# Pooling branch of a decoder layer: input projected channel-major, window sums by shifted additions on VectorE, stored rows transposed back

## The chip, the cores and the metric

One core of a Trainium2 chip runs the whole kernel. The metric is the device time of one execution in microseconds. The kernel before took 1297.56 us (median of 3 runs, 1297.35 to 1298.0).

## The reference, cut to what matters

One decoder layer over 264 token rows (256 of a prompt, 8 single-token samples), D = 1024, float32:

```
h = rmsnorm(x);  z = h @ w_in                       # q, f, v, g, u, gate_a, gate_b, 1024 columns each
u -> ext = [15 older rows (zero for the prompt) ; u]
for group g, window w in (2, 4, 8, 16), 256 channels each:
    d  = sum(last w rows of ext) / min(pos + 1, w) - u
    y_pool = (d @ w_pool[g]) * pool_scale
merged = sigmoid(gate_a) * o + sigmoid(gate_b) * y_pool       # o: output of the HGRN2 heads
x += merged @ w_out;  x += top-4-of-32 experts(rmsnorm(x));  x += gated embedding;  final rmsnorm
new_pool = the last 15 rows of ext                            # an output of its own
```

## The kernel before, in words

Each engine has one instruction stream, written out by hand, and semaphores tie them. `bank_jobs` lists every use of the eight PSUM banks in the order in which TensorE (`pe`) fills them, with the engine that drains each ("a" ScalarE, "v" VectorE). `wait_filled` waits for a place in that order, `begin` for the drain of the bank's user before, `wait_drained` for the count of drains of one engine. Where `step` is used, VectorE or GpSimd waits for its own instruction before the next.

The weights `w_in` come as 14 chunks of 512 columns (2 MB each) into four slots. q and f are projected channel-major (L751: weights stationary, 264 tokens moving). The others are projected token-major (`chunk`, L705: 128 tokens stationary, 512 columns moving; `sample_rows`, L728: the 8 sample rows, in four column groups of bank 4). In the stretch that the change touches, TensorE does in order:

- four `state_steps` (L816), beside each of which stand up to four k-steps of the two `u` chunks (L826), and the eight `o` products (L835, L844);
- the last k-step of the u chunks and `gb` chunk 0 (L705), the sample rows of u and gb in one call with 512 columns (L728), `gb` chunk 1 (L705);
- `dT` (L863 to L865): for each of eight channel blocks, u rows times a band matrix of 1/w weights minus identity gives the pooled difference, channel-major; a third product with `selw` adds the sample rows and their 15 older rows (`bufrows`). Each dT bank is copied out by ScalarE or VectorE (L1457, L1786);
- `yp` (L873, L884): dT times `w_pool`; then the transposes `mT` of the merged rows (L666 by `turn_rows`), the product with w_out for the samples (L912), for tile 0 (L905) and for tile 1 (L929), the router, and the experts.

GpSimd makes the constants, the band matrices too (L542 to L551), and only then issues the eight loads of the sample state, `s0` (L564). Later it multiplies sigmoid(gate_b) by pool_scale, one instruction for each of three tiles (L604), once ScalarE has drained gb chunk 1. VectorE waits for all three (L1788), then for each tile in the order samples, 0, 1 multiplies the yp banks by gb (L1794) and adds to og (L1796), which releases that tile's mT.

SyncE's queue issues the weight loads in a fixed order. Expert weights are pieces ("granules") of 1 MB in a ring of 16; `load_first` waits for `s_used`, which TensorE raises as it is done with memory: eight times in dT (L863), four times in the transposes of tile 1, six in L973, then with each pair of pieces consumed.

Two experts make a `pair`, 16 pairs in all: gather rows (L1058, L1068), gate and up products, down product (all L1147), combine (L1205).

Of the kernel before, what the change touches and what calls it, by code (L numbers as in the profile page):

```python
# [14 lines left out]
P = 128  # L15
D = 1024
# [37 lines left out]
def bank_jobs():  # L54
# [62 lines left out]
def build(nc, x_prompt, x_sample, p_prompt, p_sample, state_hgrn, state_pool, g_mix, w_in,  # L117
# [14 lines left out]
    with ExitStack() as ctx:  # L132
# [77 lines left out]
        u = rows3(HG)  # L210
# [5 lines left out]
        pscale_b = view(G0, D)  # L216
        wpool = view(G12, 2048).rearrange("p (g k n) -> p g k n", g=4, k=2)
        wout = view(R + 8 * GRAN, 8192).rearrange("p (k n) -> p k n", k=KD)
        band0 = [view(BAND + g * 144, 144) for g in range(4)]
        band1 = [view(BAND + 4 * 144 + g * P, P) for g in range(4)]  # L220
# [85 lines left out]
        s_ust = sem("pooling_rows_stored")  # L306
        s_gbs = sem("pool_gate_scaled")
# [103 lines left out]
        def _(sp):  # L411
# [53 lines left out]
            sp.wait_ge(s_snew, NS)  # L465
            sp.dma_start(wpool, w_pool[0].rearrange("g (k p) n -> p g k n", p=P)).then_inc(ld["wpool"], 16)

            wait_filled(sp, ("o", 1, 1))
# [40 lines left out]
        def _(pool):  # L509
# [31 lines left out]
            for g, w in enumerate(WINDOWS):  # L541
                step(pool.memset(band0[g], 1.0 / w))  # L542
                for t in range(w - 1):
                    pool.memset(band0[g][:, t:t + 1], 1.0 / (t + 1))
                step(pool.memset(band1[g], 1.0 / w))
                for m, n in ((band0[g], 144), (band1[g], P)):
                    step(pool.affine_select(out=m, in_=m, compare_op=ALU.is_ge, fill=0.0, base=0,
                                            pattern=[[1, n]], channel_multiplier=-1))
                    step(pool.affine_select(out=m, in_=m, compare_op=ALU.is_ge, fill=0.0, base=w - 1,
                                            pattern=[[-1, n]], channel_multiplier=1))  # L550
                    step(pool.tensor_tensor(m[:, 0:P], m[:, 0:P], ident, ALU.subtract))  # L551

                m = selw[:, g, :]
                step(pool.memset(m, 1.0 / w))
                step(pool.affine_select(out=m, in_=m, compare_op=ALU.is_ge, fill=0.0, base=-(NS + BUF + 1 - w),
                                        pattern=[[-BUF, 8]], channel_multiplier=1))
                step(pool.affine_select(out=m, in_=m, compare_op=ALU.is_ge, fill=0.0, base=NS + BUF - 1,
                                        pattern=[[BUF, 8]], channel_multiplier=-1))
                step(pool.tensor_scalar(m[0:NS], ident[0:NS, 0:NS], 1.0 / w - 1.0, None, ALU.mult))
# [32 lines left out]
            pool.dma_start(bufrows[NS:P], rows_of).then_inc(ld["bufrows"], 16)  # L592
            pool.dma_start(new_hgrn_prompt[0, 0].rearrange("h k v -> k h v"), state[NCH]).then_inc(s_stst, 16)

            wait_drained(pool, ("u", 0, 1))
            wait_drained(pool, ("u", 1, 1))
            pool.dma_start(new_pool_prompt[0, 0], u[P - BUF:P, 1, :]).then_inc(s_ust, 16)
            wait_drained(pool, ("u", "s", 3))
            pool.dma_start(new_pool_sample[0, :, BUF - 1, :], bufrows[0:NS]).then_inc(s_ust, 16)
# [7 lines left out]
            wait_filled(pool, ("dT", KD - 1))  # L607
# [3 lines left out]
            pool.wait_ge(s_ust, 32)  # L611
# [43 lines left out]
        def _(pe):  # L655
# [167 lines left out]
            beside = [(n, k) for n in range(2) for k in range(KD - 1)]  # L823
# [30 lines left out]
            for name in [("u", n, t) for n in range(2) for t in range(2)] + [("u", "s", 3)]:  # L854
                wait_drained(pe, name)
            pe.wait_ge(ld["bufrows"], 16)
            pe.wait_ge(s_const, 2)
            for c in range(KD):
                name, g = ("dT", c), c // 2
                begin(name)  # L860
                o, cc = job_bank(name), slice(c * P, (c + 1) * P)

                pe.matmul(o[:, 0:144], u[:, 0, cc], band0[g], start=True, stop=True, skip_group_check=True).then_inc(s_used, 1)  # L863
                pe.matmul(o[:, P:SEQ], u[:, 1, cc], band1[g], start=False, stop=True, skip_group_check=True)
                ins = pe.matmul(o[:, SEQ:T], bufrows[:, cc], selw[:, g, :], start=True, stop=True)  # L865
                fill_done(ins, name)
            pe.wait_ge(ld["wpool"], 16)
            for c in range(KD):
                wait_drained(pe, ("dT", c))
            begin(("yp", 2, 0))  # L870
            for k in range(2):
                for g in range(4):
                    ins = pe.matmul(piece(("yp", 2, g)), dT[:, 2 * g + k, toks(2)], wpool[:, g, k, :],  # L873
                                    start=(k == 0), stop=(k == 1))
                    if k == 1:
                        fill_done(ins, ("yp", 2, g))
# [417 lines left out]
        def _(act):  # L1294
# [126 lines left out]

            for t in range(2):
# [10 lines left out]
            act.wait_ge(s_qm, 1)  # L1433
            copy_out(("u", 0, 0), u[:, 0, halves(0)], job_bank(("u", 0, 0))[:, :])
            copy_out(("u", 1, 0), u[:, 0, halves(1)], job_bank(("u", 1, 0))[:, :])
# [14 lines left out]
            for j in range(4):  # L1450
                name = ("u", "s", j)
                wait_filled(act, name)
                dst = bufrows[0:NS, halves(j)] if j < 2 else gb[0:NS, 2, halves(j % 2)]
                drain_done(act.activation(dst, bank[4][32 * j:32 * j + NS, :], ACT.Copy if j < 2 else ACT.Sigmoid), name)
            pool_gate(1)
            for c in range(0, KD, 2):
                copy_out(("dT", c), dT[:, c, :], job_bank(("dT", c))[:, 0:T])  # L1457
# [130 lines left out]
        def _(dve):  # L1588
# [183 lines left out]
            dve.wait_ge(s_qm, 1)  # L1772
            copy_out(("u", 0, 1), u[:, 1, halves(0)], job_bank(("u", 0, 1))[:, :])
            copy_out(("u", 1, 1), u[:, 1, halves(1)], job_bank(("u", 1, 1))[:, :])

# [9 lines left out]
            for c in range(1, KD, 2):  # L1785
                copy_out(("dT", c), dT[:, c, :], job_bank(("dT", c))[:, 0:T])  # L1786
# [289 lines left out]
```

## Time and profile before

| | us |
|---|---|
| median of 3 runs | 1297.56 |
| profiled execution, its own time | 1297.42 |
| span of its trace | 1295.7 |
| TensorE matmul busy | 1225.1 (95% of the span) |
| TensorE weight loads busy | 554.1 (43%) |
| VectorE / ScalarE / GpSimd busy | 331.4 / 175.2 / 73.8 |
| loaded from memory | 455.00 MB, 356 GB/s over the span |

The span is counted from the first to the last record; the execution's own time is 1.72 us longer. A time such as 249.13 below is counted in us from the start of the span. A matmul of float32 stands as two instructions in the trace. Busy time of pipelined matmuls overlaps, so durations of TensorE work are best read from one start to the next.

### The profile page before, as it was taken

What the parts mean: (1) busy time and instruction counts of PE and PEld (TensorE: products, weight loads), DVE (VectorE), ACT (ScalarE), POOL (GpSimd) and SP (SyncE); (2) the same over time, 40 slices, a digit from 0 to 9 for tenths busy, and PEclk for the clock granted to TensorE, in tenths of its full rate; (3) what the DMA queues carried; (4) which work ended last, traced back from release to release, by engine and by line L of the source; (5) the groups of instructions that cost most, each with busy time, mean ns of one, the idle gap of its engine ahead of it and who ended that gap; (6) DMA issues with size and microseconds to landing.
All of it is one profiled execution on the core that took longest, in us unless ns stands there. A gap on an engine that the chain in (4) does not pass through costs nothing.

```text
span 1295.7 us, 15572 instructions
## 1 busy us (share of the span) xinstructions
PE 1225.1 (95%) x6203; PEld 554.1 (43%) x6203; DVE 331.4 (26%) x648; ACT 175.2 (14%) x435; POOL 73.8 (6%) x168
## 2 busy tenths in 40 slices
PE   7999999999999999999898999989898989999996
PEld 6855445556333343433334343433333343434333
DVE  3155344133311212212121221211121212212223
ACT  3136203121100100001010000000010100001022
POOL 8021020210000000000000000000000000000001
PEclk9999999999999999999999999999999999999998
DMA  9847272595889999999999999999999999999961
GB/s 333 291 144 252 82 285 83 201 375 223 358 355 422 422 420 421 421 422 422 422 422 422 422 422 422 422 423 422 422 422 422 422 422 422 422 421 422 420 263 36
DMA packets 80051, 461.55 MB, mean 356 GB/s; under 512 B 8181, under 2 KB 9377, under 8 KB 31112
## 3 DMA queue, kind: packets, MB, share of 16 engines
q1 hardware_dynamic: 74512, 445.18, 84.0%
q0 software_dynamic: 3424, 11.28, 2.8%
q10 hardware_dynamic: 2072, 4.49, 1.1%
q8 instruction: 30, 0.49, 0.2%
q14 instruction: 13, 0.11, 0.0%
HBM read 455.00 MB, written 6.39 MB: 356 GB/s over the span
## 4 chain that ended last, share of the span: by engine, by line
PE 74%; DMA 22%; DVE 2%; issue 1%; SPq 0%; ACT 0%; POOLq 0%; POOL 0%; DVEq 0%; ACTq 0%
PE bank L1147 37%; DMA arena<-in_w_down_dram 19%; PE bank L705 11%; PE bank L1205 5%; PE bank L751 4%; PE bank L1058 3%; PE bank L1241 2%; DMA arena<-in_w_up_dram 2%; PE bank L1068 1%; DMA arena<-in_w_ple_gate_dram 1%; PE bank L728 1%; PE bank L1168 1%; PE bank L929 1%; PE bank L905 1%; DVE arena L1961 1%; PE bank L1076 1%
## 5 line engine op out<-in xcount | busy, mean ns | idle before, releaser
L1147 PE MATMUL bank<-arena 128*64 128x512 f32 x3072 | 679.1, 596 | 37.8 <-DMA arena<-in_w_up_dram 24.6
L1147 PEld LDWEIGHTS bank<-arena 128*64 128x64 f32 x3072 | 222.9, 137 | 475.2 <-issue 472.5
L705 PE MATMUL bank<-arena 128*128 128x512 f32 x320 | 140.0, 595 | 0.0
L705 PEld LDWEIGHTS bank<-arena 128*128 128x128 f32 x320 | 60.0, 190 | 74.6 <-issue 73.9
L1973 DVE TENSOR_TENSOR arena<-bank,arena 128x512 f32<-128x512 f32 (+1 forms) x96 | 61.6, 682 | 75.5 <-PE bank L1205 75.3
L1205 PE MATMUL bank<-arena 128*128 128x512 f32 (+1 forms) x192 | 74.6, 601 | 0.9 <-DVE arena L1966 0.9
L1058 PEld LDWEIGHTS bank<-arena 128*128 128x128 f32 x512 | 62.7, 196 | 25.4 <-issue 25.2
L1955 DVE TENSOR_SCALAR arena<-bank 128x512 f32<-128x512 f32 x32 | 20.6, 686 | 196.6 <-PE bank L1147 196.6
L1966 DVE COPY arena<-bank 128x512 f32<-128x512 f32 x16 | 11.1, 692 | 230.7 <-PE bank L1147 230.7
L1058 PE MATMUL bank<-arena 128*128 128x128 f32 x512 | 68.8, 288 | 0.0
L1937 DVE TENSOR_SCALAR arena<-bank 128x512 f32<-128x512 f32 x32 | 20.6, 686 | 182.6 <-PE bank L1147 182.6
L751 PE MATMUL bank<-arena 128*128 128x264 f32 x256 | 57.2, 386 | 0.6 <-DVE arena L1631 0.6
L1489 ACT ACTIVATE arena<-arena 128x1024 f32<-128x1024 f32 x16 | 16.9, 1057 | 281.2 <-DVE arena L1937 281.2
L635 POOL TENSOR_SCALAR arena<-arena 128x1 f32<-128x1 f32 (+1 forms) x3 | 0.7, 219 | 944.2 <-ACT arena L1524 944.2
L751 PEld LDWEIGHTS bank<-arena 128*128 128x128 f32 x256 | 48.6, 190 | 8.9 <-ACT arena L1349 0.7
L1474 ACT ACTIVATE arena<-bank,arena 128x128 f32<-128x128 f32 x124 | 33.7, 382 | 54.9 <-PE bank L1068 54.9
L1205 PEld LDWEIGHTS bank<-arena 128*128 128x128 f32 (+1 forms) x192 | 24.7, 155 | 38.0 <-issue 36.2
L1503 ACT ACTIVATE arena<-bank 128x512 f32<-128x512 f32 x16 | 9.6, 597 | 231.5 <-PE bank L1147 231.5
L1501 ACT ACTIVATE arena<-bank 128x264 f32<-128x264 f32 x16 | 6.3, 391 | 249.3 <-PE bank L1191 249.3
L1241 PE MATMUL bank<-arena 128*8 128x256 f32 (+2 forms) x144 | 31.7, 452 | 1.7 <-DMA arena<-in_w_ple_gate_dram 1.7
L1076 PE MATMUL bank<-arena 128*128 128x128 f32 x128 | 19.6, 296 | 11.5 <-DVE arena L1961 11.5
L1940 DVE TENSOR_TENSOR arena<-arena 128x1024 f32<-128x1024 f32 x16 | 19.6, 1225 | 19.1 <-ACT arena L1489 19.1
(253 smaller groups left out, 705.1 us busy)
## 6 DMA issues: line engine op xcount, KB each, us to landing
arena<-in_w_gate_dram SPq DMA_DIRECT2D x128, 1024.0 KB, 26.5
arena<-in_w_up_dram SPq DMA_DIRECT2D x128, 1024.0 KB, 26.5
arena<-in_w_down_dram SPq DMA_DIRECT2D x126, 1024.0 KB, 26.1
arena<-in_w_in_dram SPq DMA_DIRECT2D x14, 2048.0 KB, 12.4
out_dram<-arena POOLq DMA_DIRECT2D x9, 512.0 KB, 5.2
arena<-in_state_hgrn_dram POOLq DMA_DIRECT2D x8, 512.0 KB, 12.7
arena<-sample_values ACTq DMA_DIRECT2D x8, 512.0 KB, 7.2
arena<-in_w_out_dram SPq DMA_DIRECT2D x4, 1024.0 KB, 8.0
```

The costliest lines, as they stand in the source:

```text
L705: ins = pe.matmul(job_bank(name)[:, :], hT[:, k, toks(t)], w[:, k, :], start=(k == 0), stop=(k == KD - 1))
L751: ins = pe.matmul(job_bank((kind, h))[:, 0:T], w_slot[c % NSLOT][:, k, (h % 4) * P:(h % 4 + 1) * P], hT[:, k, :], start=(k == 0), stop=(k ...
L1058: ins = pe.matmul(XG[k // 4][:, (k % 4) * P:(k % 4 + 1) * P], h2[:, t, every_other(k)], oh[:, t, :], start=(k % 4 == 0 and t == 0), stop=F ...
L1076: ins = pe.transpose(out[c][:, j * P:(j + 1) * P], src[:, every_other(k)], ident)
L1147: ins = pe.matmul(out[c][hp(one), :], src[:, k * P + CAP * one:k * P + CAP * one + CAP], w[one][:, j, halves(c)], start=(first and k == 0) ...
L1205: ins = pe.matmul(out, comb[:, toks(t)], y_sb[:, halves(c)], start=True, stop=True)
L1241: ins = pe.matmul(gate_piece(r, t, n), xT[:, k, toks(t)], gran[k // 2][:, k % 2, gate_cols(t, n)], start=(k == 0), stop=(k == KD - 1))
L1474: ins = act.activation(xT_e[:, k * P:(k + 1) * P], bank[6 + c][:, (k % 4) * P:(k % 4 + 1) * P], ACT.Copy, scale=gffn[:, k:k + 1])
L1937: ins = dve.tensor_scalar(g_sb[:, halves(c)], bank[c][:, :], LIMIT, None, ALU.min)
L1940: dve.tensor_tensor(g_sb, g_sb, sig_sb, ALU.mult).then_inc(s_dloop, 1)
L1955: ins = dve.tensor_scalar(u_sb[:, halves(c)], bank[2 + c][:, :], LIMIT, -LIMIT, ALU.min, ALU.max)
L1973: ins = dve.tensor_tensor(xs, src, xs, ALU.add)
```

## The change

- The `u` chunks are computed channel-major: eight `uT` jobs, each 8 matmuls of 128x264 as for q and f, two of them beside each `state_steps`; ScalarE copies each to `uT` with 16 columns of room ahead of it. `sample_rows` is called for gb alone, with 256 columns. The bands, dT matmuls and dT copies are gone.
- New on TensorE, between the sample rows of gb and gb chunk 1: `bs` (eight products of older sample rows with `selw`, 8 columns each) and `ur` (eight transposes of the 23 rows to be stored, back to token-major); ScalarE copies ur out.
- New on VectorE: window sums by additions of shifted copies, 1, 2, 3 and 4 for the four windows, the scaling by 1/w and subtraction of u, the first w-1 columns with their own divisors, and the sample columns.
- yp waits for that chain (`s_pooled`). The first eight expert pieces are released together by the first yp matmul.
- The load of w_pool moves behind `o`; piece 0 no longer waits for L604; the wait for the stored rows moves behind it.
- GpSimd's constants get shorter, and what stands behind them is issued earlier.

```diff
 # bank_jobs
-    for t in range(2):
-        for half in range(2):
-            jobs += [(("dS", t, half, c), 4 + c, "v") for c in range(4)]
+    for n in range(4):
+        jobs += [(("dS", n // 2, n % 2, c), 4 + c, "v") for c in range(4)]
+        jobs += [(("uT", c), c % 4, "a") for c in (2 * n, 2 * n + 1)]
...
-    chunk("u", 0, 0, "av")
-    chunk("u", 1, 1, "av")
     chunk("gb", 0, 0, "aa")
-    jobs += [(("u", "s", j), 4, "a") for j in range(4)]
+    jobs += [(("gb", "s", j), 4, "a") for j in range(4)]
+    jobs.append((("bs",), 5, "v"))
+    jobs += [(("ur", half), 6 + half, "a") for half in range(2)]
     chunk("gb", 1, 1, "aa")
-    for c in range(KD):
-        jobs.append((("dT", c), c % 4, "av"[c % 2]))
 # sync
+            wait_filled(sp, ("o", 1, 1))
             sp.dma_start(wpool, ...).then_inc(ld["wpool"], 16)
...
-            sp.wait_ge(s_ust, 32)
-            for n, at_ in enumerate((1, 2, 3, 4, 5, 6, 15, 16)):
-                load_first(at_, n + 1)
-            sp.wait_ge(s_gbs, NT)
+            for at_ in (1, 2, 3, 4, 5, 6, 15, 16):
+                load_first(at_, 8)
             sp.wait_ge(s_osq, 1)
             load_first(0, 8)
+            sp.wait_ge(s_ust, 32)
 # gpsimd: constants, for each window
-                step(pool.memset(band0[g], 1.0 / w))
+                step(pool.memset(share[:, g, :], 1.0 / w))
                 for t in range(w - 1):
-                    pool.memset(band0[g][:, t:t + 1], 1.0 / (t + 1))
-                step(pool.memset(band1[g], 1.0 / w))
-                for m, n in ((band0[g], 144), (band1[g], P)):
-                    (two affine_select and one tensor_tensor)
+                    pool.memset(share[:, g, t:t + 1], 1.0 / (t + 1))
 # tensor
             for n in range(4):
                 state_steps(n // 2, n % 2)
-                for m, k in beside[4 * n:4 * n + 4]:
-                    chunk_step("u", m, k)
+                for c in (2 * n, 2 * n + 1):
+                    name, w = ("uT", c), w_slot[chunk_no[("u", c // 4)] % NSLOT]
+                    begin(name)
+                    for k in range(KD):
+                        ins = pe.matmul(job_bank(name)[:, 0:T], w[:, k, (c % 4) * P:(c % 4 + 1) * P], hT[:, k, :], ...)
+                    fill_done(ins, name)
...
-            for n in range(2):
-                chunk_step("u", n, KD - 1)
             chunk("gb", 0)
-            sample_rows("u", (10, 11, 12, 13))
-            chunk("gb", 1)
+            sample_rows("gb", (12, 13))
+            begin(("bs",))
             for c in range(KD):
-                (two band products and one with selw)
+                ins = pe.matmul(bank[5][:, c * NS:(c + 1) * NS], bufrows[0:NS * BUF, c * P:(c + 1) * P],
+                                selw[0:NS * BUF, c // 2, :], start=True, stop=True)
+            fill_done(ins, ("bs",))
+            (waits for all uT drains; ur: 8 transposes of uT[:, c, 16 + SEQ - BUF:16 + T] into banks 6 and 7)
+            chunk("gb", 1)
             pe.wait_ge(ld["wpool"], 16)
+            pe.wait_ge(s_pooled, 1)
 # scalar, ahead of the o jobs
+            act.wait_ge(s_snew, NS)
+            for c in range(KD):
+                copy_out(("uT", c), uT[:, c, 16:16 + T], job_bank(("uT", c))[:, 0:T])
 # vector
+            step(dve.memset(uT[:, :, 0:16], 0.0))
+            wait_filled(dve, ("bs",))
+            for g, w in enumerate(WINDOWS):
+                two, src, shift = slice(2 * g, 2 * g + 2), uT[:, 2 * g:2 * g + 2], 1
+                for n in range(g + 1):
+                    lo = 2 * shift - 1
+                    step(dve.tensor_tensor(sums[n % 2][:, :, lo:272], src[:, :, lo:272], src[:, :, lo - shift:272 - shift], ALU.add))
+                    src, shift = sums[n % 2], 2 * shift
+                step(dve.scalar_tensor_tensor(dT[:, two, 0:SEQ], src[:, :, 16:272], 1.0 / w, uT[:, two, 16:272], ALU.mult, ALU.subtract))
+                step(dve.tensor_tensor(src[:, :, 16:15 + w], ..share.., ALU.mult))
+                step(dve.tensor_tensor(dT[:, two, 0:w - 1], src[:, :, 16:15 + w], uT[:, two, 16:15 + w], ALU.subtract))
+                ins = dve.scalar_tensor_tensor(dT[:, two, SEQ:T], uT[:, two, 16 + SEQ:16 + T], 1.0 / w - 1.0, ..bank[5].., ALU.mult, ALU.add)
+            drain_done(ins, ("bs",))
+            dve.memset(stat[:, 30:31], 0.0).then_inc(s_pooled, 1)
```

## Rows read from the trace of the kernel before

**Rows 1.** The page: busy tenths of the DMA engines in 40 slices.

```profile
DMA  9847272595889999999999999999999999999961
```

**Rows 2.** Windows: stretch, length, busy time of each engine, granted clock, DMA share, GB/s.

```profile
290.00:300.00 10.00, 10.00 (x67) 5.52 (x66) 3.56 (x17) 0.00 (x0) 0.00 (x0) 1.00 0.08 32
500.00:1000.00 500.00, 467.89 (x2315) 189.37 (x2313) 103.01 (x153) 35.18 (x90) 0.00 (x0) 1.00 1.01 422
```

**Rows 3.** Timeline of SyncE's queue: start, length, line, what it issues, count.

```profile
249.62 3.74 SPq L434 DMA_DIRECT2D arena<-in_w_gate_dram  x6
302.18 1.98 SPq L434 DMA_DIRECT2D arena<-in_w_up_dram  x4
316.93 17.01 SPq L434 DMA_DIRECT2D arena<-in_w_down_dram  x6
```

**Rows 4.** Timeline of TensorE, 173 to 269 us: start, length, line, shapes, count, idle before.

```profile
174.63 7.13 PE L705 MATMUL bank<-arena 128*128 128x512 f32 x16
181.69 1.17 PE L816 MATMUL bank<-arena 32*128 32x128 f32 x32
199.13 3.27 PE L705 MATMUL bank<-arena 128*128 128x512 f32 x7
202.67 1.05 PE L835 MATMUL bank<-arena 128*128 128x128 f32 x8
210.95 17.43 PE L705 MATMUL bank<-arena 128*128 128x512 f32 x40
228.31 7.05 PE L728 MATMUL bank<-arena 128*8 128x512 f32 x64
235.30 14.00 PE L705 MATMUL bank<-arena 128*128 128x512 f32 x32
249.13 0.41 PE L863 MATMUL bank<-arena 128*128 128x144 f32 x2
255.45 1.05 PE L873 MATMUL bank<-arena 128*8 128x256 f32 x16 [0.72 <-DVE arena L1599]
263.54 1.68 PE L666 MATMUL bank<-arena 8*128 8x8 f32 x16
265.14 3.64 PE L912 MATMUL bank<-arena 128*8 128x256 f32 x64
268.71 1.09 PE L666 MATMUL bank<-arena 128*128 128x128 f32 x8
```

**Rows 5.** TensorE elsewhere: the nearest rows to the new jobs.

```profile
12.58 57.20 PE L751 MATMUL bank<-arena 128*128 128x264 f32 x256 [0.63 <-DVE arena L1631]
303.51 1.94 PE L956 MATMUL bank<-arena 128*128 128x32 f32 x16
```

**Rows 6.** VectorE's groups by form: busy, mean ns of one.

```profile
L1687 DVE TENSOR_TENSOR arena<-arena 128x512 f32<-128x512 f32 x4 | 2.8, 693 | 21.2 <-ACT arena L1380 21.1
L1870 DVE SCALAR_TENSOR_TENSOR arena<-bank,arena 128x32 f32<-128x32 f32 x2 | 0.5, 251 | 1.0 <-PE bank L956 1.0
```

**Rows 7.** Timeline of GpSimd.

```profile
25.30 7.32 POOL L564 DMA_DIRECT2D arena<-in_state_hgrn_dram  x8
250.08 6.97 POOL L604 TENSOR_TENSOR arena<-arena 8x1024 f32<-8x1024 f32 x3 [11.47 <-ACT arena L1447]
```

**Rows 8.** Timeline of VectorE around the merge.

```profile
257.08 1.77 DVE L1794 TENSOR_TENSOR arena<-bank,arena 8x256 f32<-8x256 f32 x4 [1.89 <-POOL arena L604]
258.88 1.22 DVE L1796 TENSOR_TENSOR arena<-arena 8x1024 f32<-8x1024 f32 x1
261.45 1.22 DVE L1796 TENSOR_TENSOR arena<-arena 128x1024 f32<-128x1024 f32 x1
```

**Rows 9.** The window in which the granted clock falls.

```profile
325.00:330.00 5.00, 5.00 (x18) 1.42 (x16) 0.00 (x0) 0.00 (x0) 0.00 (x0) 0.66 0.37 154
```

**Rows 10.** Timeline of TensorE, products of the first pair, outside and inside that stretch.

```profile
313.21 7.09 PE L1147 MATMUL bank<-arena 128*64 128x512 f32 x32
324.80 8.78 PE L1147 MATMUL bank<-arena 128*64 128x512 f32 x32 [1.29 <-ACT arena L1474]
```

More of the change, by code:

```diff
@@ L209, in build @@
         tmp = [view(TMP + n * HALF, HALF) for n in range(2)]
-        u = rows3(HG)
+        uT = view(G0, KD * (T + 16)).rearrange("p (k t) -> p k t", k=KD)
+        sums = [view(BAND, 544).rearrange("p (k t) -> p k t", k=2),
+                view(G0 + KD * (T + 16), 544).rearrange("p (k t) -> p k t", k=2)]
+        share = view(BAND + 1024, 64).rearrange("p (g t) -> p g t", g=4)
+        urows = view(HG + 2048, D, BUF + NS)
         gb = rows3(HG + 3072)
@@ L215, in build @@
         bufrows = view(V, D)
-        pscale_b = view(G0, D)
-        wpool = view(G12, 2048).rearrange("p (g k n) -> p g k n", g=4, k=2)
+        pscale_b = view(V + D, D)
+        wpool = view(HG, 2048).rearrange("p (g k n) -> p g k n", g=4, k=2)
         wout = view(R + 8 * GRAN, 8192).rearrange("p (k n) -> p k n", k=KD)
-        band0 = [view(BAND + g * 144, 144) for g in range(4)]
-        band1 = [view(BAND + 4 * 144 + g * P, P) for g in range(4)]
         h2 = rows3(OG)
@@ L306, in build @@
         s_ust = sem("pooling_rows_stored")
+        s_pooled = sem("pooled_rows_ready")
         s_gbs = sem("pool_gate_scaled")
@@ L822, in _ @@
             wait_chunk(chunk_no[("u", 1)])
-            beside = [(n, k) for n in range(2) for k in range(KD - 1)]
             for n in range(4):
                 state_steps(n // 2, n % 2)
-                for m, k in beside[4 * n:4 * n + 4]:
-                    chunk_step("u", m, k)
+                for c in (2 * n, 2 * n + 1):
+                    name, w = ("uT", c), w_slot[chunk_no[("u", c // 4)] % NSLOT]
+                    begin(name)
+                    for k in range(KD):
+                        ins = pe.matmul(job_bank(name)[:, 0:T], w[:, k, (c % 4) * P:(c % 4 + 1) * P], hT[:, k, :],
+                                        start=(k == 0), stop=(k == KD - 1))
+                    fill_done(ins, name)
             for t in range(2):
@@ L847, in _ @@
                     fill_done(ins, name)
-            for n in range(2):
-                chunk_step("u", n, KD - 1)
             chunk("gb", 0)
-            sample_rows("u", (10, 11, 12, 13))
-            chunk("gb", 1)
-            for name in [("u", n, t) for n in range(2) for t in range(2)] + [("u", "s", 3)]:
-                wait_drained(pe, name)
+            sample_rows("gb", (12, 13))
             pe.wait_ge(ld["bufrows"], 16)
             pe.wait_ge(s_const, 2)
+            begin(("bs",))
             for c in range(KD):
-                name, g = ("dT", c), c // 2
+                ins = pe.matmul(bank[5][:, c * NS:(c + 1) * NS], bufrows[0:NS * BUF, c * P:(c + 1) * P],
+                                selw[0:NS * BUF, c // 2, :], start=True, stop=True)
+            fill_done(ins, ("bs",))
+            for c in range(KD):
+                wait_drained(pe, ("uT", c))
+            for half in range(2):
+                name = ("ur", half)
                 begin(name)
[L861 to L865, printed above, removed]
+                for j in range(4):
+                    ins = pe.transpose(job_bank(name)[0:BUF + NS, j * P:(j + 1) * P],
+                                       uT[:, 4 * half + j, 16 + SEQ - BUF:16 + T], ident)
                 fill_done(ins, name)
+            chunk("gb", 1)
             pe.wait_ge(ld["wpool"], 16)
-            for c in range(KD):
-                wait_drained(pe, ("dT", c))
+            pe.wait_ge(s_pooled, 1)
             begin(("yp", 2, 0))
@@ L874, in _ @@
                                     start=(k == 0), stop=(k == 1))
+                    if k == 0 and g == 0:
+                        ins.then_inc(s_used, 8)
                     if k == 1:
@@ L1420, in _ @@
             gate_chunk("ga", 1)
+            act.wait_ge(s_snew, NS)
+            for c in range(KD):
+                copy_out(("uT", c), uT[:, c, 16:16 + T], job_bank(("uT", c))[:, 0:T])
             for t in range(2):
@@ L1450, in _ @@
             for j in range(4):
-                name = ("u", "s", j)
+                name = ("gb", "s", j)
                 wait_filled(act, name)
-                dst = bufrows[0:NS, halves(j)] if j < 2 else gb[0:NS, 2, halves(j % 2)]
-                drain_done(act.activation(dst, bank[4][32 * j:32 * j + NS, :], ACT.Copy if j < 2 else ACT.Sigmoid), name)
+                drain_done(act.activation(gb[0:NS, 2, cols(2, j)], bank[4][32 * j:32 * j + NS, 0:256], ACT.Sigmoid), name)
+            for half in range(2):
+                name = ("ur", half)
+                copy_out(name, urows[:, halves(half)], job_bank(name)[0:BUF + NS, :])
             pool_gate(1)
-            for c in range(0, KD, 2):
-                copy_out(("dT", c), dT[:, c, :], job_bank(("dT", c))[:, 0:T])
             turned("mT", mT, ORD)
```

46 lines of the change are left out of this document (20 added, 26 removed).

## The prediction

> **What bounds the kernel now.** Read first the DMA line of the page [rows 1]: from the thirteenth slice on (some 390 us) the DMA engines are always busy. The windows say it sharper [rows 2]: over 500 us in the experts the DMA share is 1.01 at 422 GB/s while TensorE is busy 467.89, so it waits for weights. The experts are bound by the stream of pieces, whose bytes the change leaves alone. But before the stream closes up it has gaps: from 290 to 300 us the DMA share is 0.08 with TensorE busy all of the time [rows 2], and SyncE issues the next pieces at 302.18 and 316.93 only because TensorE has come that far [rows 3]. Up to there TensorE's order of work sets the time; whatever it is earlier at the product after the pooling (265.14, L912), the stream and the end are earlier too. So the timeline of TensorE from 173 to 269 us [rows 4] is what has to be worked out anew, and the two engines that release its merged rows, GpSimd and VectorE [rows 7, 8].
>
> **The change part by part, TensorE up to the end of gb chunk 1.**
> - u as uT. One uT job is 16 of the instructions of L751, 57.20 / 256 = 0.223 us each [rows 5]; the pair of jobs beside a `state_steps` takes 32 x 0.223 = 7.15 us. The four k-steps that stand there now take 181.69 - 174.63 = 7.06 [rows 4]. Three times +0.09: +0.27. Beside the fourth there are two k-steps now, 202.67 - 199.13 = 3.54; in their place 7.15: +3.61. The u k-steps behind the o products go: 228.31 - 210.95 = 17.36 less a chunk of 235.30 to 249.13 = 13.83, so -3.53.
> - Sample rows. 64 instructions of 512 columns take 235.30 - 228.31 = 6.99; with 256 columns the same count is 3.6 (L912, from 265.14 to 268.71 it is 3.57) [rows 4]: -3.42.
> - bs. 16 instructions with 128x128 weights and 8 columns. No such row stands alone. The nearest has 32 columns: 1.94 us for 16 [rows 5], that is 1.8 without the last one's tail. At least half of that, and at most one of L705's slots each (13.83 / 32 = 0.43, 6.9 in all) bound it; I take +1.8.
> - ur. Eight transposes; eight of 128x128 take 1.09 with their tail [rows 4]. Between 0.5 and 2.2 for 23 rows out instead of 128; I take +1.0.
>
> The sum is +0.27 + 3.61 - 3.53 - 3.42 + 1.8 + 1.0 = -0.3: gb chunk 1 ends at 248.8 instead of 249.13. The banks that uT takes (0 to 3) are drained by ScalarE, which has no other job between ga chunk 1 and o; its copies come in pairs, one pair in some 8 us. So the new work on TensorE replaces the old one for one, and what is gained lies behind gb chunk 1.
>
> **Behind gb chunk 1.** dT and the wait for its last copy go: 255.45 - 249.13 = 6.32 us [rows 4]. yp can start at 248.8, if VectorE's chain is done, and as it took 263.54 - 255.45 = 8.09, it ends at 256.9.
>
> **VectorE's chain** starts when bs is filled, at 248.8 - 13.83 - 1.0 = 234.0. It has 10 additions of two blocks (542 to 514 elements, mean 536), each 536 / 512 x 0.693 = 0.725 [rows 6]: 7.25. Four scalings with subtraction, 512 elements, 0.70 each: 2.8. Twelve small ones at the 0.25 of L1870 [rows 6]: 3.0. Each waits for the one before; the gap between dependent ones is 0.03 (257.08 + 1.77 to 258.88) [rows 8], 27 times 0.9. Sum 14.0, so the pooled columns are ready at 248.0, 0.8 us before TensorE asks. Gb chunk 1 and the ur transposes (14.8 us) hide it; in the order written, VectorE has no other work there. Without that cover it would cost all of its 14 us. Bounds: 10 us, if the small ones cost nearly nothing, and 21 if a wait of a step costs 0.3.
>
> **What is late next.** The merge. GpSimd begins L604 at 250.08, when ScalarE has drained gb chunk 1, and takes 6.97 us for its three tiles [rows 7]; VectorE waits for it even now, 1.89 us, and starts at 257.08 [rows 8]. None of this moves but with the end of gb chunk 1, by 0.3. So VectorE starts at 256.8, releases the sample tile at 256.8 + 1.77 + 0.03 + 1.22 = 259.8, and tile 0 at 261.45 + 1.22 - 0.34 = 262.3, as by then the yp banks have long been full. TensorE, done at 256.9, waits 2.9 us, turns the sample rows in 0.6, waits until 262.4, and turns tile 0 in 1.0. L912 starts at 263.4 instead of 265.14: **1.7 us** of the 6.6 are left. Tile 1's merge (two banks and one addition, about 2.6 us) is done at 265, before L912 ends at 267; behind that, the order and the distances are those of before.
>
> **The queues.** w_pool (1 MB) is loaded behind o instead of at 174; yp comes over 30 us later: nothing. In SyncE's queue it stands ahead of w_out only by its issue. The first eight pieces are issued now from 249.62 on [rows 3], one by one with dT, and afterwards in one burst when yp has begun, at 249; piece 0 follows without waiting for L604. The gap of 290 to 302 shows 11 us of slack before the next ones are due, which are asked for 1.7 earlier: nothing. The stored rows go out over GpSimd's queue around 237, with 6 us until piece 7 needs them gone and no engine waiting behind them but L604, 12 us later. The load of bufrows is issued when o has been drained, now 3.6 us later (some 218); bs asks at 232: nothing. The constants of GpSimd shorten: `s0` is issued at some 12 us instead of 25.30 [rows 7]; as TensorE is held by nothing but its own work from 12.58 on, no gain; the risk is a rival.
>
> The sum against the profiled execution is 1297.42 - 1.7 = 1295.7; the median of the three runs is 0.14 above that execution, so I forecast **1295.8 us**.
>
> **The rivals.**
 The new stretch, 256.9 to 262.4, has 4.9 us of waiting in 5.5, and L912 behind it has only 8 columns per group. Against it: the transposes and L912 run there today at full clock. If it falls, and lasts as long as at 325, half of it lies in the stall: 0.9 to 1.7 lost, 1296.7 to 1297.5. **The slower end of it:** if the low clock stays for all of mT 0, L912 and mT 1 (1.0 + 3.6 + 1.0), it costs 5.6, and the time is 1297.5 + 3.9 = 1301.4. It decides for slower from a loss of 1.7 us. The Trainium skill (TensorE: Matmul & The Clock Gate, The HAM clock gate) says that idleness of the array lowers its clock and sustained work restores it; by that rule the fall in this stall is the expected case.
> 2. *The dip at 325 goes away*, since all of it is shifted by 1.7 us against whatever decides it. That gives back 1.7 more: 1294.1. For: it is one dip, after one short wait of 1.29 [rows 10]. Against: the three runs lie within 0.65 us, so it is not a thing of chance.
> 3. *GpSimd's scaling does not hold the merge* (VectorE starts as soon as yp is full): all 6.6 come off, 1290.9. Against it stands the wait of 1.89 for L604 [rows 8].
> 4. *VectorE's chain is too long.* TensorE's yp may start up to 251.7 without any loss, since the merge holds it anyway, and has lost all gain at 255.4: a chain of 21 us where I count 14. From there on slower, up to 1298. By the Trainium skill (SBUF — State Buffer, Who interferes with whom), a VectorE instruction with two SBUF inputs and a GpSimd one lock each other out. No row here shows it, as they do not overlap now; by my sum the chain ends 1.7 us before L604 starts.
> 5. *The earlier s0 loads (4 MB) starve w_in.* The second chunk of q is due at 12.58 + 14.3 = 26.9. If it comes later by more than 1.7 the kernel gets slower; say 2 to 4 us late, 1298 to 1300. Against it: even if all of s0 went first, the input tiles (1 MB), two chunks and s0 are 9.4 MB, 22 us at the 422 GB/s of [rows 2], behind the start of the loads near 1 us. It is close only if the small pieces of s0 move much slower: unlikely, and the later chunks have 14 us more each.
>
> **How the numbers follow.** The forecast has a chance of 0.42, the first rival 0.28, the second 0.14, the third 0.04, the fourth 0.04, the fifth 0.04, other things 0.04. What the measurement can tell from no change is about 0.2%, 2.6 us: below 1295.0 is faster, above 1300.2 slower. Faster: the second and third rival and the low edge of the first case (0.04), 0.21. Slower: the tail of the first rival 0.05, of the last ones 0.04, 0.09. Same: 0.70. The range, 1293.6 to 1299.2, takes in the second rival and the first up to a loss of 3.4, and leaves out the third and the far tails.
>
> **What would show it right or wrong.** In the changed trace: L912's counterpart starts at about 263.4; the last gb chunk ends within 1 us of 248.8; TensorE has two waits for VectorE's merge of 2.9 and 2.0 us, and VectorE one for GpSimd ahead of it; the three GpSimd scalings still take 2.34 each; the chain on VectorE lasts 14 us and yp waits less than 1 for it; the granted clock is 1.00 from 255 to 275. It is wrong if L912 starts later than 264.5, if the stream of pieces does not close up earlier by what L912 gained, or if a wait appears before 173 us.

## The result

The changed kernel took 1301.63 us (median of 18 runs) against 1298.12 for the kernel before (18 runs, 1297.35 to 1299.94). Seventeen of the 18 lie between 1298.45 and 1304.0, and a single slow one of 4454.66 is left out of the ratio, which is 1.002 with a 95% interval of 1.0013 to 1.0028. The two medians alone are 3.5 us (0.27%) apart. It is slower by 0.2 to 0.3%. The forecast was 1295.8 with a range to 1299.2: wrong in sign, and outside the range. The profiled execution took 1301.44 us with a span of 1299.7, 4.0 more than before.

### The profile page after: what moved, and what is told of

Its sections match the earlier page's. It is cut to its first block, busy times and chain, and to the rows that moved or that the text cites. A ratio compares the mean times of both kernels' runs of the same rounds, so it can differ in the third digit from the quotient of the medians.

```text
span 1299.7 us, 15644 instructions
## 1 busy us (share of the span) xinstructions
PE 1224.4 (94%) x6243; PEld 565.8 (44%) x6243; DVE 340.3 (26%) x670; ACT 175.8 (14%) x439; POOL 63.0 (5%) x136
## 4 chain that ended last, share of the span: by engine, by line
PE 73%; DMA 22%; DVE 2%; POOL 1%; issue 1%; SPq 1%; ACT 0%; POOLq 0%; DVEq 0%; ACTq 0%
PE bank L1139 36%; DMA arena<-in_w_down_dram 19%; PE bank L692 9%; PE bank L1197 5%; PE bank L738 5%; PE bank L1050 3%; PE bank L1233 2%; PE bank L816 2%; DMA arena<-in_w_up_dram 2%; PE bank L1060 1%; DMA arena<-in_w_ple_gate_dram 1%; PE bank L1160 1%; PE bank L715 1%; PE bank L921 1%; PE bank L897 1%; DVE arena L1970 1%
## 5 line engine op out<-in xcount | busy, mean ns | idle before, releaser
L1139 PE MATMUL bank<-arena 128*64 128x512 f32 x3072 | 678.8, 596 | 38.0 <-DMA arena<-in_w_up_dram 24.8
L692 PE MATMUL bank<-arena 128*128 128x512 f32 x256 | 111.4, 594 | 0.0
L692 PEld LDWEIGHTS bank<-arena 128*128 128x128 f32 x256 | 48.1, 190 | 59.9 <-issue 59.6
L1050 PEld LDWEIGHTS bank<-arena 128*128 128x128 f32 x512 | 62.7, 196 | 25.4 <-issue 25.2
L738 PE MATMUL bank<-arena 128*128 128x264 f32 x256 | 59.3, 396 | 0.6 <-DVE arena L1623 0.6
L738 PEld LDWEIGHTS bank<-arena 128*128 128x128 f32 x256 | 50.0, 196 | 9.6 <-issue 0.7
L1289 ACT ACTIVATE arena<-bank 128x512 f32<-128x512 f32 (+4 forms) x32 | 15.0, 484 | 111.6 <-PE bank L816 30.6
```

The lines of the kernel that those rows point to most:

```text
L692: ins = pe.matmul(job_bank(name)[:, :], hT[:, k, toks(t)], w[:, k, :], start=(k == 0), stop=(k == KD - 1))
L738: ins = pe.matmul(job_bank((kind, h))[:, 0:T], w_slot[c % NSLOT][:, k, (h % 4) * P:(h % 4 + 1) * P], hT[:, k, :], start=(k == 0), stop=(k ...
L1050: ins = pe.matmul(XG[k // 4][:, (k % 4) * P:(k % 4 + 1) * P], h2[:, t, every_other(k)], oh[:, t, :], start=(k % 4 == 0 and t == 0), stop=F ...
L1139: ins = pe.matmul(out[c][hp(one), :], src[:, k * P + CAP * one:k * P + CAP * one + CAP], w[one][:, j, halves(c)], start=(first and k == 0) ...
```

## The profile after

The page of the changed kernel, its busy times and granted clock in 40 slices:

```profile
PE 1224.4 (94%) x6243; PEld 565.8 (44%) x6243; DVE 340.3 (26%) x670; ACT 175.8 (14%) x439; POOL 63.0 (5%) x136
PEclk9999999989999999999999999999999999999999
```

TensorE is as busy as before, GpSimd 11 us less, VectorE 9 more, and the slice from 260 to 292 us has a lower clock (the 8), which it has not in the profile before. The timeline of TensorE (start, length, line, shapes, count, idle before) shows the rest; it answers to [rows 4, 5]:

```profile
13.00 59.29 PE L738 MATMUL bank<-arena 128*128 128x264 f32 x256 [0.63 <-DVE arena L1623]
...
175.98 1.17 PE L803 MATMUL bank<-arena 32*128 32x128 f32 x32 [0.15 <-issue]
177.08 7.39 PE L816 MATMUL bank<-arena 128*128 128x264 f32 x32
184.40 1.17 PE L803 MATMUL bank<-arena 32*128 32x128 f32 x32
...
231.78 3.64 PE L715 MATMUL bank<-arena 128*8 128x256 f32 x64
235.35 1.95 PE L845 MATMUL bank<-arena 120*128 120x8 f32 x16
237.16 1.03 PE L854 MATMUL bank<-arena 128*23 128x128 f32 x8
238.03 13.90 PE L692 MATMUL bank<-arena 128*128 128x512 f32 x32
251.86 1.05 PE L863 MATMUL bank<-arena 128*8 128x256 f32 x16
252.84 7.17 PE L876 MATMUL bank<-arena 128*128 128x256 f32 x32
262.77 0.88 PE L653 MATMUL bank<-arena 8*128 8x8 f32 x8 [2.76 <-DVE arena L1805]
265.35 1.97 PE L653 MATMUL bank<-arena 128*128 128x128 f32 x8 [1.70 <-DVE arena L1805]
267.25 4.89 PE L904 MATMUL bank<-arena 128*8 128x256 f32 x64
272.07 1.09 PE L653 MATMUL bank<-arena 128*128 128x128 f32 x8
```

Three things stand there. The q and f projections (L738) take 2.1 us more than before, 59.22 from the first start to the next group (72.22) against 57.12, and begin 0.4 later. From the first `state_steps` (173.53 before, 175.98 now) to the sample product (265.14, 267.25) it is 91.27 us against 91.61: 0.3 gained, where 1.7 was forecast. And the two waits for the merge (2.76 and 1.70) are followed by work at half speed: the transposes of tile 0 take 1.90 from start to start, the sample product 4.82 where it was 3.57 before. The windows (length, busy times, granted clock, DMA share, GB/s) show the clock there. The kernel before, first, has 1.00 in the same stretch:

```profile
260.00:265.00 5.00, 5.00 (x33) 4.26 (x31) 4.54 (x7) 0.41 (x2) 1.10 (x3) 1.00 1.01 411
265.00:270.00 5.00, 5.00 (x75) 2.78 (x74) 1.73 (x4) 1.49 (x4) 2.97 (x7) 1.00 1.03 379
```

```profile
255.00:260.00 5.00, 5.00 (x24) 4.07 (x22) 0.30 (x1) 0.00 (x0) 5.00 (x4) 1.00 1.02 424
260.00:265.00 5.00, 0.89 (x9) 0.79 (x8) 4.81 (x8) 0.22 (x1) 5.00 (x11) 0.80 1.00 417
265.00:270.00 5.00, 4.65 (x36) 2.61 (x40) 2.71 (x4) 1.19 (x2) 0.00 (x0) 0.52 1.05 321
270.00:275.00 5.00, 5.00 (x53) 2.69 (x46) 1.68 (x4) 2.12 (x4) 0.00 (x0) 1.00 0.99 322
```

The clock has two levels, 1.2 and 2.4 GHz, and 0.80 and 0.52 are means over 5 us. Together they lack 0.20 x 5 + 0.48 x 5 = 3.4 us of full speed. The dip at 325 us in the kernel before [rows 9] lacks half as much, 0.34 x 5 = 1.7.

What holds the merge is, as forecast, GpSimd's scaling (L592), which VectorE awaits for 9.68 us. The first of these lines is the last of VectorE's chain; they answer to [rows 7, 8]:

```profile
249.97 0.06 DVE L1795 MEMSET arena<- 128x1 f32 x1
259.70 1.76 DVE L1803 TENSOR_TENSOR arena<-bank,arena 8x256 f32<-8x256 f32 x4 [9.68 <-POOL arena L592]
261.50 1.21 DVE L1805 TENSOR_TENSOR arena<-arena 8x1024 f32<-8x1024 f32 x1
```

```profile
252.71 6.96 POOL L592 TENSOR_TENSOR arena<-arena 8x1024 f32<-8x1024 f32 x3 [12.54 <-ACT arena L1439]
```

The chain runs from 237.41 to 250.03: 12.6 us, and yp does not wait for it.

## The experiments

**Fill the waits, leave them in place.**

```diff
-            turn_rows("mT", og, ..., tiles=(2, 0))
+            wait_drained(pe, ("gb", 1, 1))
+            for _ in range(5):
+                pe.matmul(bank[3][:, 0:256], ident, hT[:, 0, 0:256], start=True, stop=True)
+            turn_rows("mT", og, ..., tiles=(2,))
+            for _ in range(3):
+                (the same product)
+            turn_rows("mT", og, ..., tiles=(0,))
```

> The changed kernel with dummy products (128x256) in TensorE's two waits for the merge: five before the transposes of the sample rows (2.2 of 2.76 us), three before those of tile 0 (1.3 of 1.70 us). The waits themselves stay. Theory A (the clock falls to 1.2 GHz because of these waits, and the transposes and the sample product run slowly behind them): the clock stays at 1.00 from 255 to 275, the transposes of tile 0 take 1.0 instead of 1.90 and the sample product 3.57 instead of 4.82, the time falls by about 2.1 us to 1299.5. Theory B (the loss is made at the start of the kernel, where the q and f projections take 59.3 instead of 57.2 us since constants are shorter and the state loads earlier): no change, about 1301.6.

Measured: 1298.74 us (12 runs, 1294.46 to 1305.43), against 1299.12 for the kernel before beside it (23 runs), ratio 1.0004 (0.9987 to 1.0021): not told apart from the kernel before. Its timeline of TensorE:

```profile
248.95 1.05 PE L863 MATMUL bank<-arena 128*8 128x256 f32 x16
...
262.43 1.09 PE L653 MATMUL bank<-arena 128*128 128x128 f32 x8 [0.43 <-DVE arena L1811]
263.45 3.64 PE L910 MATMUL bank<-arena 128*8 128x256 f32 x64
267.02 1.09 PE L653 MATMUL bank<-arena 128*128 128x128 f32 x8
```

The merge is no earlier, but the work behind it runs at full speed: 1.02 and 3.57. This is the world that was forecast: gb chunk 1 ends at 248.95 (forecast 248.8) and the sample product starts at 263.45 (forecast 263.4). So the fall of the clock in the stall is caused by TensorE having nothing to do there, and costs 0.9 + 1.25 = 2.1 us. The Trainium skill (TensorE: Matmul & The Clock Gate, The HAM clock gate) says that an idle array loses its clock. The trace agrees: 1.90 and 4.82 us behind the empty waits, 1.02 and 3.57 behind the filled ones.

The other executions say the same. The mean granted clock of a whole execution is 0.998 in 5 of these 12, and never above 0.994 in the 37 comparable executions of kernels that have this merge unfilled.

The time is less clear than the trace. The interval of this ratio overlaps that of the changed kernel (1.0013 to 1.0028), so the expected fall of 2.1 us fits but isn't shown by the times. In this execution the clock fell in the router stretch instead, the thin products between the w_out product and the first pair of experts (windows of the same run, where the kernel before has 1.00):

```profile
300.00:305.00 5.00, 4.90 (x41) 4.27 (x39) 3.20 (x10) 3.61 (x5) 0.90 (x4) 1.00 0.73 247
305.00:310.00 5.00, 5.00 (x22) 4.13 (x21) 3.13 (x11) 0.68 (x3) 1.75 (x6) 0.51 1.00 424
```

**Wait for one tile's scaling at a time.**

```diff
-            dve.wait_ge(s_gbs, NT)
             for t in ORD:
+                dve.wait_ge(s_gbs, ORD.index(t) + 1)
```

> The changed kernel, but VectorE waits only for the scaling of the tile that it merges next, not for all three. Step of the prediction tested: the three GpSimd scalings of 6.97 us hold the merge. Then VectorE starts 4.65 us earlier, both waits of TensorE (2.76 and 1.70) all but go, the sample product starts at about 262 instead of 267.25 and the clock does not fall: some 5.5 us from the waits and 1.3 from its full speed, about 1295. If the clock falls all the same (theory A wrong in its cause): about 1296.5. If the merge is held by something else: no change, 1301.6.

Measured: 1295.05 (12 runs, 1291.17 to 1298.72), ratio to before 0.9968 (0.9956 to 0.9981). By the intervals it is faster than both kernels, by 0.3% against the one before.

```profile
249.04 1.05 PE L863 MATMUL bank<-arena 128*8 128x256 f32 x16
250.02 7.17 PE L876 MATMUL bank<-arena 128*128 128x256 f32 x32
257.12 0.66 PE L653 MATMUL bank<-arena 8*128 8x8 f32 x8
259.03 1.09 PE L653 MATMUL bank<-arena 128*128 128x128 f32 x8 [1.25 <-DVE arena L1805]
260.05 3.64 PE L904 MATMUL bank<-arena 128*8 128x256 f32 x64
```

The scaling did hold the merge. The sample product starts at 260.05, 2 us earlier than expected. That the time still came out at 1295 is in part luck, as in this execution the clock fell in the router stretch (0.65 and 0.67 over 300 to 310). One wait of 1.25 is left, for the most part because VectorE and GpSimd now get in each other's way. GpSimd's three instructions take 7.99 us in place of 6.96, and two of VectorE's additions 1.61 and 1.95 in place of 1.21:

```profile
252.27 1.76 DVE L1803 TENSOR_TENSOR arena<-bank,arena 8x256 f32<-8x256 f32 x4 [5.07 <-POOL arena L592]
254.06 1.61 DVE L1805 TENSOR_TENSOR arena<-arena 8x1024 f32<-8x1024 f32 x1
255.70 1.29 DVE L1803 TENSOR_TENSOR arena<-bank,arena 128x512 f32<-128x512 f32 x2
257.02 1.95 DVE L1805 TENSOR_TENSOR arena<-arena 128x1024 f32<-128x1024 f32 x1
```

**Load the sample state late.** `wait_filled(pool, ("q", 3))` ahead of L554.

> The changed kernel, but GpSimd issues the loads of the sample state only when four q heads are done (at about 28 us, near the 25.3 of before, instead of 17.7). Theory B with the loads as cause: the q and f projections take 57.2 us again and the time falls by about 2 us, to 1299.6. Theory A: no change, about 1301.6; the length of the first q head then varies between executions whatever the loads do.

Measured: 1303.01 (6 runs, 1301.37 to 1304.53), ratio 1.0034 (1.0021 to 1.0046). q and f took 60.13. The slow start is there with the loads late as well, so the early loads are not what slows it.

**Both, with filler in the first pair.** The wait for each tile, and `keep_warm(2, bank[5])` behind `gather_samples((1,))`.

> As the one with a wait for each tile, and with two dummy products of 128x256 in the first expert pair, in TensorE's wait of 1.29 us ahead of which 32 products take 8.6 to 8.8 instead of 7.09 us. If that fall of the clock comes from the wait: 1.6 us less than without them, about 1293.4. If it comes from the thin products before it (128x128 and 8 rows): no difference, about 1295, or 0.2 more where the dummies outlast the wait.

Measured: 1293.67 (6 runs, 1291.56 to 1296.05), ratio 0.9963 (0.9949 to 0.9977). The 32 products take 7.02 from start to start. That alone doesn't show that the filler did it, as they took 7.01 without it in the run with only the wait for each tile. In this one the clock fell behind the short wait of the merge, though it is only 1.23 us:

```profile
258.73 1.09 PE L653 MATMUL bank<-arena 128*128 128x128 f32 x8 [1.23 <-DVE arena L1806]
259.75 5.33 PE L904 MATMUL bank<-arena 128*8 128x256 f32 x64
```

**The same filler at the start, in both kernels.** Eleven products before the first transposes:

```diff
             pe.wait_ge(s_const, 1)
+            for _ in range(11):
+                pe.matmul(bank[6][:, 0:P], ones, ident, start=True, stop=True)
```

> The kernel before, with 11 dummy products (128x128, ones times identity) on TensorE from about 2 us until the first rows are normalised, near 7 us. Theory A2: in some executions TensorE still runs at 1.2 GHz for the first head or two of q (6 instructions in 2 us instead of 11 between 13 and 17 us, seen in the changed kernel and in the one with late state loads, not in the one before), and that is chance of the clock, the same for both kernels. Then with this work ahead the first q heads are always fast: the median of before falls by 0 to 1 us, to 1297.5, and its spread shrinks. Theory B2 (start of the changed kernel is slow by its own doing): no change of before, 1298 to 1299.

> The changed kernel with the same 11 dummy products. Theory A2: q and f take 57.1 us and the time falls by about 2 us, to 1299.5; what is left against the kernel before with the same work is the fall of the clock in the stall less the order's gain, +0.5 to +1.5. Theory B2: q and f still take 59 us or more and the time stays at 1301.6.

Measured, beside 30 runs of the kernel before at 1299.67: the kernel before with it 1298.13 (12 runs), ratio 0.9991 (0.9981 to 1.0002); the changed kernel with it 1301.27 (12 runs, 1297.73 to 1306.04), ratio 1.0016 (1.0003 to 1.0028). q and f took 57.13 in both profiles. The changed kernel without filler was not run beside these, and the kernel before stood 1.5 us higher here than beside its 1301.63, so what the filler gives the changed kernel can't be read from the two medians. What can be read is that with the start filled in both, the changed kernel is still 3.1 us slower: the start is not what sets the two kernels apart.

The filler seems to help the kernel before too. Below 1299 us lie 7 of its 12 executions with filler and 7 of the 30 without. That speaks for a slow start by chance in both kernels (theory A2), though the interval of the ratio takes in 1 and no profile caught it in the kernel before. The two profiled executions, both with a fast start, differ by 1.0 us (spans 1295.3 and 1296.3), which is the stall's clock against the order's gain. These windows show the slow start in the changed kernel; the granted clock of the view says 1.00, but only 5 and 6 instructions (in brackets) stand in 2 us in place of 11.
```profile
13.00:15.00 2.00, 2.00 (x5) 1.59 (x6) 1.05 (x6) 1.66 (x3) 0.00 (x0) 1.00 0.78 257
15.00:17.00 2.00, 2.00 (x6) 1.58 (x5) 0.00 (x0) 0.00 (x0) 0.00 (x0) 1.00 1.08 390
```

**All three parts.** Filler at the start, the wait for each tile, filler in the first pair.

> The changed kernel with the dummy products at the start, VectorE's wait for each tile alone, and the two dummy products in the first expert pair. All parts together: the sample product starts at about 260 as in the run with the wait for each tile, the clock is high in the q heads and in the first pair: 1292.5, with 1.5 to 3 us more where the clock falls elsewhere between 258 and 310.

Measured: 1293.38 (7 runs, 1292.51 to 1298.69) against 1299.67 beside it, ratio 0.9963 (0.9947 to 0.9979). It has the lowest median, but the same ratio as the one without filler at the start, and is not told apart from it.

**Scale what can be scaled early.** On top of all three parts, GpSimd does the sample tile and the first halves beside VectorE's chain. `scale(t, n)` is the old scaling of tile t, cut to half n (2 stands for the whole row).

```diff
+            scale(2, 2).then_inc(s_gbs, 1)
+            scale(0, 0)
+            scale(1, 0)
             wait_drained(pool, ("gb", 1, 1))
+            scale(0, 1).then_inc(s_gbs, 1)
+            scale(1, 1).then_inc(s_gbs, 1)
```

> As the one before it, but GpSimd scales the sample tile and the first halves of tiles 0 and 1 as soon as gb chunk 0 and the sample rows are drained, beside VectorE's chain of shifted additions, and only the second halves (1.2 us each) behind gb chunk 1. Theory of no contention: GpSimd's rows keep 2.34 and 1.2 us, VectorE's chain stays at 12.6 us, TensorE's last wait of 1.25 us at the merge of tile 0 goes, about 1 us less than without it (1291.5). Theory of a lock between GpSimd and VectorE instructions with two inputs in SBUF (the Trainium skill, SBUF — State Buffer, Who interferes with whom): additions that meet a GpSimd instruction last up to 2.3 us longer, the chain takes 15 to 17 us, ends after gb chunk 1, and yp starts 1 to 3 us late: no gain, or up to 1 us slower.

Measured: 1297.62 (12 runs, 1296.6 to 1303.32), ratio 0.999 (0.9979 to 1.0), 4 us slower than the version before it, where at most 1 was expected. VectorE's chain and GpSimd's rows:

```profile
234.16 0.72 DVE L1791 TENSOR_TENSOR arena<-arena 128x542 f32<-128x542 f32 x1 [10.84 <-PE bank L853]
...
236.13 4.96 DVE L1791 TENSOR_TENSOR arena<-arena 128x542 f32<-128x542 f32 x2
241.13 1.64 DVE L1794 SCALAR_TENSOR_TENSOR arena<-arena 128x512 f32<-128x512 f32 x1
...
251.41 1.13 DVE L1796 TENSOR_TENSOR arena<-arena 128x30 f32<-128x30 f32 x1
...
253.04 0.06 DVE L1804 MEMSET arena<- 128x1 f32 x1
```

```profile
236.94 5.27 POOL L592 TENSOR_TENSOR arena<-arena 8x1024 f32<-8x1024 f32 x3
249.39 3.11 POOL L592 TENSOR_TENSOR arena<-arena 128x512 f32<-128x512 f32 x2 [7.18 <-ACT arena L1448]
```

```profile
253.45 1.89 PE L871 MATMUL bank<-arena 128*8 128x256 f32 x16 [4.77 <-DVE arena L1804]
```

Two additions of 0.73 each became 4.96; a product of 30 elements took 1.13 in place of 0.19; the chain took 18.9 us in place of 12.6, and yp waited 4.77 for it. The Trainium skill (SBUF — State Buffer, Who interferes with whom) says that a VectorE instruction with two inputs in SBUF contends with a GpSimd instruction that reads SBUF. The trace agrees, and at 18.9 us the chain is longer than the 15 to 17 expected of it.

This run also bears on what the filler in the first pair does. Its sample product starts at 264.57, and that of a second profile of the kernel before at 264.58, so TensorE reaches the 32 products at the same time in both. The kernel before first:

```profile
324.24 8.78 PE L1147 MATMUL bank<-arena 128*64 128x512 f32 x32 [1.29 <-ACT arena L1474]
```

```profile
324.22 7.09 PE L1148 MATMUL bank<-arena 128*64 128x512 f32 x32 [0.23 <-ACT arena L1475]
```

With the wait filled the dip at 325 is gone. It is gone in all three profiles that have this filler, and there in 10 of the 11 that don't. The two kernels differ ahead of this stretch, so the pair alone is no proof; together with the count it is strong evidence.

**More profiles of both kernels, unaltered.**

> The changed kernel unaltered, for one more profile. Open is where its executions of 1301 to 1304 us lose what the profiled ones with a fast start do not. Theory A: the clock falls in every execution in the merge's waits (transposes of tile 0 1.9 us, sample product 4.8 to 5.5), and beside it in some at the start (q and f over 59 us) or in the router stretch (12.6 us between the first logits of tile 1 and the first pair's products, in place of 9.7): each execution's span is 1296.3 plus 2 to 3 us for each of these. Rival: work other than TensorE's slow clock (a wait for DMA) makes the difference.

> As the one before it: the merge's fall of the clock in every execution, the other places by chance, the span 1296.3 plus 2 to 3 us for each. Rival: a wait for DMA.

> The kernel before unaltered, for one more profile. Theory A: no fall of the clock from 249 to 275 us, where TensorE has no wait over 0.72 us; span 1295.7, or 2 to 3 us more where the start or the router stretch falls. If the slow start belongs to the changed kernel alone (theory B), q and f take 57.2 us here.

> As the one before it. Together with it: if one of the two has the slow start, it is chance for both kernels.

Measured, beside the first profiles (us; each from one start to the next; "router" is from the first logits of tile 1 to the first pair's products):

| | span | q and f | sample product | router |
|---|---|---|---|---|
| before | 1295.7 | 57.12 | 3.57 | 9.70 |
| before, again | 1295.9 / 1295.2 | 57.13 / 57.13 | 3.57 / 3.57 | 9.69 / 9.69 |
| changed | 1299.7 | 59.22 | 4.82 | 9.69 |
| changed, again 1 | 1304.1 | 58.88 | 4.53 | 12.64 |
| changed, again 2 | 1296.4 | 57.13 | 4.84 | 9.69 |

Windows of the changed kernel's slowest profile ("again 1", 1305.88 us) show its falls:

```profile
260.00:265.00 5.00, 1.01 (x8) 0.92 (x8) 4.84 (x8) 0.22 (x1) 4.77 (x11) 0.72 1.00 415
265.00:270.00 5.00, 4.88 (x48) 2.77 (x52) 2.48 (x4) 1.20 (x2) 0.00 (x0) 0.60 1.02 316
...
310.00:315.00 5.00, 5.00 (x19) 4.29 (x19) 2.95 (x10) 0.23 (x2) 1.35 (x5) 0.50 1.01 428
```

The clock falls in the merge in every one of the five profiles that have the changed kernel's merge as it is (4.53 to 5.39 for the sample product). Beside it some have a slow start, and some a fall in the router stretch. This one has a slow first gate product at the end too: its 16 instructions take 8.83 us, and 7.13 in the kernel before. The rival, a wait for DMA, fell: TensorE's waits for the expert weights add up to 36.6 us in it (24.8 + 11.8) and to 36.5 in the kernel before (24.6 + 11.9).

The mean granted clock, on record for each execution and blind to the start, sorts the others. Of the changed kernel's 17, eight have 0.994, as the two profiles without a router fall, and their median is 1299.3. Nine have 0.990 or 0.991, nearer to the 0.989 of the profile with it, and theirs is 1303.1. So about half of the executions have one more fall somewhere. Of 53 executions of the kernel before, two are below 0.995. Where the extra fall lies is known only for the profiled executions.

## Why the prediction was wrong

**What held.** The stream of weights bounds the experts, and what TensorE loses before it reaches the end: the last gate products start 3.25 us later (1255.99, before 1252.74), the sample product's end 3.36 later. dT and its wait are gone. VectorE's chain hides beside gb chunk 1 (12.6 us, forecast 14.0). bs took 1.81 and ur 0.87 (1.8 and 1.0). GpSimd's scaling took over as the limit, with waits of 2.76 and 1.70 (forecast 2.9 and 2.0); with the waits filled, the sample product started 0.05 us from where the forecast had it. The queues moved nothing that shows, though the sample state was asked for at 17.71 us and not at 12. The third rival fell, as the wait on GpSimd was real. The fourth did not occur, as the chain never met the scaling, though the contention behind it exists. The fifth fell with the late-load run.

**The step that failed** is that work behind the new waits takes what it took before. The forecast turns tile 0 "in 1.0" and lets "the order and the distances" be "those of before", with the clock at 1.00 from 255 to 275. Measured were 1.90 for tile 0 and 4.53 to 5.39 for the sample product, in place of 1.0 and 3.57. The fall was seen and put down as the first rival. The prediction calls it "the expected case" and still gives it a chance of 0.28, and it occurred in five profiles of five. It was sized at 0.9 to 1.7, as a fall as long as that at 325 with half of it in the stall. It was twice as long: in the first profile 3.4 us of full speed were missing, 1.3 in the waits and 2.1 on the transposes of tile 0 and the sample product. Against 1.2 to 1.7 gained this gives about +1.0 between spans where nothing else falls. The forecast had set against it that they "run there today at full clock"; but today TensorE comes to them out of 8 us of yp with no gap.

The measured 1301.63 lies next to the 1301.4 of that rival's slower end. That is chance: 1301.4 was 5.6 us lost in the merge, where 2.1 were, and the rest was lost elsewhere.

**A size that was off:** a pair of uT jobs takes 184.40 - 177.08 = 7.32 us, forecast 7.15, and the last pair 7.22; all four together 0.6 more. The first job of each pair is the slow one; why is open. Two slips changed nothing: 27 gaps of 0.03 are 0.8 and not 0.9, and the chances for faster add up to 0.22 and not 0.21. The twelve small instructions of the chain took 0.16 to 0.19 each, not 0.25, which is most of the 1.4 us that it was shorter.

**What the forecast did not have.** The other 2.5 us of the 3.5 between the medians. The profiles and the clocks of the executions show them as more time at the low clock: late rises at the start, and one more fall in about half of the executions, which the one slow profile has in the router stretch. Of ten profiles of the changed kernel and its variants, three have the slow start (of seven without filler there) and three the slow router. Of four of the kernel before (one with filler at the start) none has either, but its times suggest the slow start. Why the router stretch falls more often is open: the products there are thin in both kernels, and what differs is when TensorE reaches them and what the clock did before. No experiment filled or moved that stretch alone. The second rival, that the dip at 325 goes away because all of it is shifted, did not occur in the changed kernel: its three profiles reach the products between 325 and 331 us and all have the dip. Where it is gone, the wait ahead of it has filler, but for the run with only the wait for each tile.

## What to carry to other kernels

Before a piece of TensorE work is taken away, look at which engine releases the work behind it: the time saved ahead of that release turns into waiting, here 4.5 of 6.3 us. Cost a new wait of more than a microsecond with the clock that it loses, on the work behind it; fill it with products nobody needs, as at 325; or wait for less, as the wait for each tile did (0.9968 of before by one moved line). Do not put GpSimd work beside a VectorE chain of additions with both inputs in SBUF, however idle GpSimd is.

## What the runs showed of the hardware

- Behind a wait as short as 1.23 us the clock fell to half (5.33 for the sample product, granted clock 0.66 over 260 to 265), and in another execution, behind a wait of 1.25 at the same place, it did not (3.64). The times of such a kernel spread: 1297.73 to 1306.04 for the changed kernel with filler at the start.
- With two dummy products in a wait of 1.29 us the clock stayed up behind it in three profiles of three: 7.09 us for the 32 products in place of 8.78, at the same time of the execution.
- The granted clock of the windows reads 1.00 in the first microseconds even where TensorE does 5 instructions in 2 us in place of 11. There the trace's first clock record, a rise, tells: 17.24 us in that profile, 11.37 in the kernel before, 6.55 with filler ahead of it.
- Where VectorE and GpSimd instructions with both inputs in SBUF meet, VectorE can lose several times its own length: 4.96 us for two additions of 0.73, 1.13 for a product of 0.19. GpSimd loses less: 7.99 us for three products in place of 6.96.
